# Expert blocks of 32 rows instead of 64, and gate_up matrices moved as one 32 KB run per partition

## The reference, cut to what matters

```python
h = modulate(x, norm_ffn[i], sh2, sc2)          # rmsnorm(x)*gain*(1+scale)+shift
idx, wts = route(h, w_router, router_bias)      # 2 experts of 32 for each token
def expert_block(xb, e):
    g, u = split(xb @ w_gu[e], 2)               # w_gu[e]: 1024 x 1024
    return (silu(g) * u) @ w_dn[e]              # w_dn[e]:  512 x 1024
x = x + g2 * sum_over_2_choices(weight * expert_row)
```

## Time and profile before

| | us |
|---|---|
| runs of the kernel before | 1861.31, 1861.31, 1865.79 (median 1861.31) |
| the profiled execution's own time | 1864.89 |
| its span in the profile | 1863.1 |
| expert stage of layer 0, first gate_up matmul to end of last down matmul | 446.8 to 971.5 |
| expert stage of layer 1, the same | 1308.0 to 1834.7 |

### The profile page before, as it was taken

The page is one execution under the profiler, slowest core; times in us unless marked ns, Lnnn a source line. Parts: engine busy times, 40 slices in busy tenths (PEclk is TensorE's granted clock), DMA queues, the critical chain, the costliest instruction groups (busy, mean ns, idle before and its releaser), DMA issues.

```text
span 1863.1 us, 19628 instructions
## 1 busy us (share of the span) xinstructions
PE 1672.7 (90%) x7263; PEld 751.8 (40%) x7263; DVE 686.3 (37%) x1120; ACT 364.7 (20%) x766; POOL 212.3 (11%) x246
## 2 busy tenths in 40 slices
PE   4999999998999999999975999785999999999983
PEld 3644777474333333333322444345333333333321
DVE  5674776754111111111114399865111111111112
ACT  3344444111111111111101333210111111111110
POOL 1001111000111111011100112100011111011100
PEclk9898999977999999999997999895999999999996
DMA  9634222576898999999974221043798999999993
GB/s 368 244 136 158 79 71 87 182 281 235 319 408 317 409 409 409 409 408 405 406 266 193 78 68 45 0 177 144 296 386 352 378 410 408 409 407 405 400 378 143
DMA packets 149379, 516.20 MB, mean 277 GB/s; under 512 B 15297, under 2 KB 27790, under 8 KB 148018
## 3 DMA queue, kind: packets, MB, share of 16 engines
q1 hardware_dynamic: 133520, 497.96, 69.0%
q0 software_dynamic: 13472, 16.85, 2.5%
q10 hardware_dynamic: 2306, 0.28, 0.1%
HBM read 515.03 MB, written 29.36 MB: 292 GB/s over the span
## 4 chain that ended last, share of the span: by engine, by line
PE 62%; DMA 23%; DVE 11%; issue 2%; ACT 2%; SPq 1%; POOLq 0%; POOL 0%; DVEq 0%; ACTq 0%
PE ps L1024 23%; DMA ring_gu<-in_moe_w_gu_dram 21%; PE ps L1037 9%; PE ps L826 3%; PE ps L941 3%; PE ps L717 3%; PE ps L853 3%; PE ps L906 2%; DVE ring_dn L1718 2%; PE ps L760 2%; PE ps L839 2%; PE ps L740 2%; PE ps L1015 2%; PE ps L788 1%; DMA ring_gu<-in_w_ada_dram 1%
## 5 line engine op out<-in xcount | busy, mean ns | idle before, releaser
L1024 PE MATMUL ps<-ring_gu,arena 128*64 128x512 f32 x2176 | 508.2, 611 | 45.3 <-DMA ring_gu<-in_moe_w_gu_dram 41.7
L1024 PEld LDWEIGHTS ps<-ring_gu,arena 128*64 128x64 f32 x2176 | 155.2, 140 | 342.0 <-issue 328.9
L1037 PE MATMUL ps<-ring_dn,arena 128*64 128x512 f32 x1088 | 245.1, 592 | 0.9 <-ACT arena L1333 0.9
L1925 DVE TENSOR_TENSOR arena<-arena,ps 128x256 f32<-128x256 f32 x88 | 37.0, 421 | 493.9 <-ACT arena L1346 493.9
L628 POOL DMA_INDIRECT ys_dram<-arena,out_idx x88 | 87.6, 995 | 918.4 <-DVE arena L1906 895.6
L1333 ACT ACTIVATE arena<-ps 128x256 f32<-128x256 f32 x88 | 33.7, 383 | 644.6 <-PE ps L1030 644.6
L1906 DVE SCALAR_TENSOR_TENSOR arena<-ps,wtab,gate_bc 128x512 f32<-128x512 f32 x88 | 66.0, 750 | 237.1 <-PE ps L1037 237.1
L1024 PE MATMUL ps<-arena 128*64 128x512 f32 x640 | 145.3, 596 | 0.3
L1037 PEld LDWEIGHTS ps<-ring_dn,arena 128*64 128x64 f32 x1088 | 77.9, 137 | 155.6 <-issue 154.2
L1895 DVE TENSOR_SCALAR arena<-ps,scale_col,shift_col 128x128 f32<-128x128 f32 x176 | 60.1, 403 | 168.6 <-PE ps L1015 168.6
L906 PE MATMUL ps<-arena 128*128 128x512 f32 x256 | 110.6, 592 | 1.0 <-ACT arena L1148 1.0
(11 more groups left out here) (306 smaller groups left out, 1694.8 us busy)
## 6 DMA issues: line engine op xcount, KB each, us to landing
ring_gu<-in_moe_w_gu_dram SPq DMA_DIRECT2D x44, 4096.0 KB, 27.6
ring_dn<-in_moe_w_dn_dram SPq DMA_DIRECT2D x44, 2048.0 KB, 19.2
arena<-in_moe_w_gu_dram SPq DMA_DIRECT2D x20, 4096.0 KB, 30.1
arena<-in_moe_w_dn_dram SPq DMA_DIRECT2D x20, 2048.0 KB, 25.7
ring_gu<-in_w_ada_dram SPq DMA_DIRECT2D x12, 2048.0 KB, 20.6
ring_gu<-in_w_ada_dram SPq DMA_DIRECT2D x48, 512.0 KB, 3.6
arena<-in_rnn_w_in_dram SPq DMA_DIRECT2D x8, 1024.0 KB, 6.5
ring_dn<-ys_dram SPq DMA_DIRECT2D x8, 1024.0 KB, 7.9
```

The source lines that it names most:

```text
L1024: last = mm(ps[s_ * ROWS:(s_ + 1) * ROWS, pb, :].rearrange("p (a b) -> p a b", a=2), rows[:, k, :], pair[:, :, s_, :], start=(k == 0), sto ...
L1037: last = mm(ps[s_ * ROWS:(s_ + 1) * ROWS, pb, :], part, w[:, f, s_ * HALF:(s_ + 1) * HALF], start=(f == 0), stop=(f == FT - 1))
```

## The change

It has five parts.

1. **Blocks of 32 rows.** `ROWS` = 32 and `TILES` = 4. `CAP` is 3, 3, 5, 4, 3, 3, 3, then 2 eleven times, then 1 fourteen times: 60 blocks, four to a unit, 15 units. In each k step of `gate_up` four matmuls of 32 stationary columns and 256 moving columns stand where two of 64 and 512 stood; `down` likewise. `hidden_transposed` is one transpose. `MAX_EXTRA` is 26. A table `column()` places blocks in 110 index columns (`NCOL`, 100 before).
2. **Gathers and scatters.** A unit is gathered by four indirect DMAs of 32 rows; a block's result is scattered as four quarter rows of 1 KB for each token row. `yo` has four buffers.
3. **gate_up as one run.** `gu_rows` puts rows 8p to 8p+7 on partition p, one contiguous run of 32 KB. Channel order follows: wherever rows of an FFN input are transposed (`norm_transposes` of 1 and 3, `rows_transposed`, `sum_columns` of those columns) the PE reads every eighth element instead of 128 neighbours.
4. **Columns and router.** `norm_ffn` and two pieces of `b_ada` are loaded by ACT's queue directly in this order, and the router matrix is loaded as `(p k)`.
5. **Index arithmetic.** Four short DVE operations more for `ncap` and two for `col_at`; seven short ones for the token tables become one.

```diff
-MAX_EXTRA = 15
+MAX_EXTRA = 26
-ROWS = 64
-CAP = [2, 2, 4] + [2] * 7 + [1] * 22
+ROWS = 32
+TILES = P // ROWS
+CAP = [3, 3, 5, 4, 3, 3, 3] + [2] * (HEAVY - TRIPLE) + [1] * (NE - HEAVY)
+        def chunk(u, k):
+            return slice(k, D, KT) if u % 2 else slice(k * P, (k + 1) * P)
         def gu_rows(l, e):
-            return moe_w_gu[l, e].rearrange("(k p) n -> p k n", p=P)
+            return moe_w_gu[l, e].rearrange("(p k) n -> p (k n)", k=KT)
...
                 def gather(t):
-                    g.indirect_dma_start(xg[:, t % 2, :], None, xn_dram, ... tok_idx[:, u:u + 1] ...)
+                    for q in range(TILES):
+                        part = slice(q * ROWS, (q + 1) * ROWS)
+                        g.indirect_dma_start(xg[part, t % 2, :], None, xn_dram, ... tok_idx[0:ROWS, col:col + 1] ...)
...
                     for k in ks:
-                        pair = w[:, k, :].rearrange("p (two s f) -> p two s f", two=2, s=2)
-                        for s_ in range(2):
+                        pair = w[:, k, :].rearrange("p (two s f) -> p two s f", two=2, s=TILES)
+                        for s_ in range(TILES):
+                            last = mm(ps[s_ * ROWS:(s_ + 1) * ROWS, pb, 0:2 * QF]..., rows[:, k, :], pair[:, :, s_, :], ...)
...
                 def down(pb, src, w):
                     for f in range(FT):
-                        for s_ in range(2):
+                        for s_ in range(TILES):
+                            last = mm(ps[s_ * ROWS:(s_ + 1) * ROWS, pb, 0:QD], src[:, f * ROWS:(f + 1) * ROWS],
+                                      w[:, f, s_ * QD:(s_ + 1) * QD], ...)
...
-                        last = tr(ps[...], xg[:, t % 2, k * P:(k + 1) * P], ident[:, :])
+                        last = tr(ps[...], xg[:, t % 2, chunk(1, k)], ident[:, :])
...
-                    if half and t + 1 < NU:
+                    if q == TILES - 2 and t + 1 < NU:
                         rows_transposed(t + 1)
```

More of the change, by code:

```diff
@@ L44, with column @@
 LRU_C = 8.0
-MAX_EXTRA = 15
+MAX_EXTRA = 26
 SKIP = 1 << 20
-ROWS = 64
-HEAVY = 10
-CAP = [2, 2, 4] + [2] * 7 + [1] * 22
[L51 to L57, removed]
+ROWS = 32
+TILES = P // ROWS
+QD = D // TILES
+QF = FE // TILES
+HEAVY = 18
+TRIPLE = 7
+CAP = [3, 3, 5, 4, 3, 3, 3] + [2] * (HEAVY - TRIPLE) + [1] * (NE - HEAVY)
+FAR_STEP = 8
+OVCOL = 84
+NCOL = OVCOL + MAX_EXTRA
+def column(o, j):
+    return o + NE * min(j, 2) + FAR_STEP * max(j - 2, 0)
+RUN = ([0, 1, 18, 7, 19, 6, 20, 8, 21, 5, 22, 9, 23, 3, 24, 10, 25, 2, 26, 27, 4]
+       + list(range(11, HEAVY)) + [28, 29, 30, 31])
+BLOCKS = [(o, j) for o in RUN for j in range(CAP[o])]
 NB = len(BLOCKS)
-assert sorted(RUN) == list(range(NU)) and len(set(BLOCKS)) == NB == sum(CAP)
+NU = NB // TILES
+assert sorted(RUN) == list(range(NE)) and NB == NU * TILES == sum(CAP)
+assert max(column(o, j) for o, j in BLOCKS) < OVCOL
+assert len({column(o, j) for o, j in BLOCKS}) == NB
 ORDER = []
@@ L558, in _ @@
             then(g.memset(keyadd[:, 1:2], 65536.0))
-            then(g.memset(phalf[0:ROWS, :], 0.0))
-            then(g.memset(phalf[ROWS:P, :], 1.0))
+            for q in range(TILES):
+                then(g.memset(pquart[q * ROWS:(q + 1) * ROWS, :], float(q)))
             for n in range(RH):
@@ L1310, in _ @@
                         hf = n % 2
-                        rows = slice(hf * ROWS, (hf + 1) * ROWS)
                         if n < 2:
@@ L1314, in _ @@
                         else:
-                            A(gate_bc[rows, 1, HALF:D], bank(g)[rows, :], ACT.Copy).then_inc(S["a_free"], 1)
+                            for q in range(2):
+                                part = slice((2 * hf + q) * ROWS, (2 * hf + q + 1) * ROWS)
+                                last = A(gate_bc[part, 1, QD:2 * QD], bank(g)[part, q * QD:(q + 1) * QD], ACT.Copy)
+                            last.then_inc(S["a_free"], 1)
                 base = NB * l
@@ L1407, in scale_out, with modulation0 @@
                                               op0=ALU.add, op1=ALU.mult)
-            def modulation0(u, stage, ch):
+            def modulation0(u, stage):
                 g = STAGES[stage]
-                b = [bcols[:, c2 * KT:(c2 + 1) * KT] for c2 in CHUNKS[ch:ch + 2]]
+                dve.wait_ge(S["ffn_in"], 32)
+                b = [bias_ffn[:, n, :] for n in range(2)]
                 shift_out(u, g, 0, b[0]).then_inc(S["d_free"], 1)
@@ L1581, in _ @@
                 else:
-                    rows = slice((n - 2) * ROWS, (n - 1) * ROWS)
-                    v.tensor_copy(gate_bc[rows, 1, 0:HALF], bank(g)[rows, :]).then_inc(S["d_free"], 1)
+                    for q in range(2):
+                        part = slice((2 * (n - 2) + q) * ROWS, (2 * (n - 2) + q + 1) * ROWS)
+                        last = v.tensor_copy(gate_bc[part, 1, 0:QD], bank(g)[part, q * QD:(q + 1) * QD])
+                    last.then_inc(S["d_free"], 1)
             def k_out(h, hb):
@@ L1837, in _ @@
                                             op0=ALU.mult, op1=ALU.add))
+                then(v.tensor_scalar(flat(over), flat(blk), 2.0, 0.0, ALU.subtract, ALU.max))
+                then(v.scalar_tensor_tensor(out=flat(col_at), in0=flat(over), scalar=float(FAR_STEP - NE),
+                                            in1=flat(col_at), op0=ALU.mult, op1=ALU.add))
                 then(v.tensor_tensor(col_ov, blk, per_token(ovb), ALU.add))
```

231 lines of the change are left out of this document (109 added, 122 removed).

## The result

The changed kernel takes 1844.1 us (median of 4 runs, 1841.8 to 1844.8) where the kernel before took 1862.1 beside it (4 runs). The ratio is 0.9897, with a 95% interval of 0.988 to 0.9915: 1.0% faster, 18 us. The forecast was a gain of 81 us and a time of 1781, with 1760 to 1834 as the range of 8 in 10. The direction is right, the size is not, and the time lies above the range. The profiled execution's own time is 1844.75 and its span 1843.0.

What follows compares the result with a forecast made beforehand. The PE was taken to bound experts with two or more blocks, the DMA those with one; afterwards the DMA alone. -56.0 + 2 - 31.4 + 4 - 9 + 9.4 = -81 us, from 1861.3 to 1781; 8 in 10: 1760 to 1834.

Steps and rivals of the forecast that it cites:

- The PE's blocks (Part 1): Expert stages: four column tiles overlap, 53.5 to 60 ns a record, 5.68 us a block, so the DMA becomes the bound.
- (b): Rival: the PE stays the bound because four tiles don't overlap or instructions aren't fed; 2162 us at 107 ns; chance 0.09.
- (c): Rival: in between, records of 75 to 85 ns on the PE, 1795 to 1910 us; chance 0.07.
- What stays idle: DMA engines while experts load: 9 us idle a layer instead of 36.1 and 37.9, saving 56.0 us in all.
- The 32 KB run (Part 3): gate_up loads: 431 instead of 409 GB/s, 9.73 us a matrix instead of 10.25, saving 31.4 us in all.
- Rival (a): The long gate_up run brings nothing and 409 GB/s stays: 1812 us; chance 0.17.
- Rival (d): Long runs load slower than 409, through neighbours 32 KB apart or packets starving GpSimd's rows: 1860 us at 380 GB/s; chance 0.10.
- Hidden or even: 60 gathers and 60 scatters take 168 us of GpSimd's 480, scatters land within four buffers; DVE operations even out: no cost.
- The strided reads: PE transposes in norms 1 and 3 reading with a stride: 2 us each, +4 in all.
- The ends: Stage ends: PE finishes 11 us after the last gate_up landing, -9 in all; 11 more extra rounds, +9.4 in all.
- The start: Stage start: three more gathers before the first transposes, +4.2 us; first gate_up matmul near 451.

Runs made afterwards that it cites:

- e2: The kernel before, still with 64-row blocks, given only the 32 KB gate_up run and its channel order: 1841.0 us beside 1864.3, ratio 0.9869.
- e5: The changed kernel with one gather of 128 rows a unit instead of four of 32, indices copied by DVE: 1815.8 us beside 1867.4, ratio 0.9719.
- e9: The changed kernel with each gather of 32 rows written to every fourth partition instead of 32 neighbouring ones: 1806.6 us beside 1866.6, ratio 0.9677.
- e14: As e9, but each gate_up matrix loaded by two DMAs in 4 KB runs to the same places: 1836.0 us beside 1865.5, ratio 0.9838.
- e1: The changed kernel with each gate_up matrix loaded by two DMAs in 4 KB runs instead of 32 KB: 1864.7 us beside 1864.3, ratio 0.9999.
- e12: As e9, with the loop of extra rounds put under one branch: 1791.5 us beside 1865.5, ratio 0.9593.
- e10: As e5, with the loop of extra rounds put under one branch: 1798.0 us beside 1866.6, ratio 0.9641.
- e7: The changed kernel without layer 1's gathers after its first two units, scatters kept: loading of layer 1 took 471.7 us against 501.4.

## Why the prediction was off, point by point

**The PE's blocks (Part 1): right.** 54 ns a record for the forecast 53.5 to 60 (and not the 67 by the ratio for three tiles), 5.58 us a block for 5.68. The rivals (b) and (c) are out. The PE's work stopped being the bound, as said.

**What stays idle: right in what remains, too large in what was there.** The fourth load went out at 470.97, 19.8 us after the first matmul where 16.7 were forecast. Over layer 0's loading the queues of the changed kernel show 197.7 MB; 500.3 - 197.7 / 0.401 leaves 7 us idle for the forecast 9. But the idle time of before was 30 us a layer, not 36. I had counted 29 down matrices and 194.6 MB. The queues of the kernel before, over layer 0's loading, show 197.2:

```profile
DMA packets 53333, 197.20 MB, mean 385 GB/s; under 512 B 5108, under 2 KB 5289, under 8 KB 53306
...
q1 hardware_dynamic: 47133, 188.59, 93.1%
q0 software_dynamic: 6173, 8.23, 4.4%
```

SyncE's 188.6 MB are 30 matrices of both kinds (188.7): the thirtieth down matrix is all but in when the last gate_up lands. 512.0 - 197.2 / 0.409 is 29.8. This term promised 6 us a layer too much.

**The 32 KB run (Part 3): right in size only without the narrow gathers.** The forecast's 9.73 us a matrix with down at 409 is 423 GB/s for the mixture. The mixture reaches 422 in e2 and e5, and 420 in e9; no window of the table's length reaches 431 or 435. In e2 the gain was 23 us, in e9 against e14 30 us. In the changed kernel it runs at 401. Rival (a), nothing from the long run, is out (e1 against the change: 19 us). Rival (d) had its outcome, a rate below 409, but not its cause: its two mechanisms were distance between neighbours' runs and long packets that hold up GpSimd's rows. It was the other way round; the rows hold up the packets, long and short.

**The step that failed: "Hidden or even".** It costed the 60 gathers a layer, four where one stood, by GpSimd's own time (168 us of 480, the scatters with them) and the scatters by their landing, and found both covered. Both were covered: PE waits for the gathers 10.4 us in all. What it left out is what a gather does while it lands to all other DMA traffic. A transfer's cost was taken as its issuing engine's time and its bytes, and where it writes wasn't asked. The price: 500.3 and 501.4 us of loading with the gathers as they are, 481.0 and 482.8 with them spread and nothing else different while the matrices load (e12; in e9, whose layer 1 stood idle longer in its first 50 us, 483.7 and 490.6). That is 19 us a layer, 38 of the 63 that are missing; the times of all runs agree, 0.9897 less 0.9677 (e9) being 41 us. Of the other 25, roughly, some 12 are the miscount above, 7 the rate of 420 for 423 (197.2 MB), and 7 idle time of 12 us a layer in the place of 9 (481.9 - 197.2 / 0.420).

The Trainium skill (SBUF — State Buffer, "Door 1: The DMA port swizzle") says that bit 6 of a partition's number picks between two sets of eight DMA ports, so that 32 or 64 partitions of one half reach eight ports and all 128 sixteen. All five placements agree with it: 128 rows, or 32 in every fourth partition, 422 and 420 GB/s; 32 neighbours, 64 neighbours, or every second of a half, 401 to 405. The prediction cited this very section, for its sentence on strided reads, and passed over the part that spoke against the change. That a narrow transfer also slows the wide ones beside it is what the runs add. That ports are the mechanism is the Trainium skill's account; the runs show the halves.

**The strided reads: nothing.** Forecast +4 (0 to 10). In the PE's timeline, 29 transposes of layer 0's norm took 5.59 us after and 4.72 before, but the granted clock was 0.59 in the one and 0.70 in the other, and time by clock is 3.3 us in both. In layer 1, with the columns start us and us, the changed kernel first and the kernel before below:

```profile
1244.49 6.11 PE L721 MATMUL ps<-ident,arena 128*128 128x128 f32 x29 [0.18 <-DVE arena L1460]
```

```profile
1252.06 6.12 PE L706 MATMUL ps<-ident,arena 128*128 128x128 f32 x29 [0.19 <-DVE arena L1445]
```

The same 29 records take the same time, at a granted clock of 0.54 in both. The prediction weighed the rule of 16-byte lines, from the same section of the Trainium skill, toward the upper end; no cost shows here.

**The ends: right.** From the last landing to the end of the last down product pass 11.4 us (947.14 to 958.57) for the forecast 11, and 15.6 before; the clock there stands at 0.50 from 946 to 950, as was reckoned with. The gap before the memset grew by 11.66 - 6.39 = 5.3 us for the forecast 4.7. What all 26 rounds cost on the path is more, the 8.5 us that e10 got back.

**The start: right in the step, lucky in the moment.** From the first gather to the first gate_up matmul pass 10.5 us (440.66 to 451.15) where 7.4 passed before (439.42 to 446.81): 3.1 more for the forecast 4.2. That the matmul came at 451.15 for the forecast 451 is luck, since this moment shifts by up to 10 us between executions.

## What to carry to other kernels

When a change cuts one transfer into narrow ones, don't cost them by their bytes and issues alone: ask which partitions each of them touches, and look at the rate of the bystanders. 32 rows into every fourth partition cost the weight loads nothing that could be measured; the same rows side by side cost 4 to 5% of the rate, which ate all that the block change brought. And a stage's byte count should be read off its queues over exactly the stretch that is divided by the rate.

## What the runs showed of the hardware that I had not expected

- Gathers whose rows all fall in one half of the partitions slow the weight loads in flight: 401 to 405 GB/s for 420 to 422, at a busy share of 1.01 in both. With 4 KB runs it is 394 for 409.
- 64 rows a gather are no better than 32 (405 GB/s and 401), though there are half as many of them.
- Sources in 1 KB pieces, read from all 128 partitions and scattered, leave the rate at 418 to 422 (e7).
- A loop of 26 empty rounds takes 8.5 us on GpSimd beyond the landing that it would wait for anyway, 15 of them 3.6 by an estimate (6.39 less 2.84); one branch around it takes all of that away.
- Four column tiles of 32 run at 54 ns a record, weight load and matmul. Holes in which the PE waited for nothing that the profile shows sum to 24.3 us before L1049 (44 of them), off the path where the DMA sets the pace.
